# Low parts one turn later on VectorE, Tanh a slot behind the taps, and two places for the levels of the inverse

## The reference

```python
# first block
x = x + hybrid_mixer(x)     # 8 heads gated delta rule + 8 heads block attention, w_in, w_out
x = x + cross_attention(x, mem)                 # 4 heads, w_xq, w_xkv, w_xo
x = x + conv_ffn(x)         # (silu(conv3(h @ w_gate) + b) * (h @ w_up)) @ w_down, width 5632
x = rmsnorm(x, final_norm_g)
# second block
x = layernorm(ALPHA * x + mamba2_mixer(x))      # a_w_in, conv4, 8 groups of state space, a_w_out
k, v = shared_kv(x)
x = layernorm(ALPHA * x + swa_mixer(x, k, v))   # b_w_in, window 128, sinks, b_w_out
```

## Time and profile before

| | |
|---|---|
| time, median of 3 runs | 2648.81 us (2643.33 to 2649.91) |
| profiled execution, its own time | 2667.62 us |
| its span | 2665.8 us |
| PE busy | 2538.2 us (95%) |
| DVE busy | 1745.6 us (65%) |
| ACT busy | 1204.4 us (45%) |
| POOL busy | 352.9 us (13%) |
| mean granted TensorE clock | 0.982 |

### The profile page before, as it was taken

The page is one execution under the profiler, slowest core; times in us unless marked ns, Lnnn a source line. Parts: engine busy times, 40 slices in busy tenths (PEclk is TensorE's granted clock), DMA queues, the critical chain, the costliest instruction groups (busy, mean ns, idle before and its releaser), DMA issues.

```text
span 2665.8 us, 51914 instructions
## 1 busy us (share of the span) xinstructions
PE 2538.2 (95%) x21076; PEld 2459.1 (92%) x21076; DVE 1745.6 (65%) x2732; ACT 1204.4 (45%) x1878; POOL 352.9 (13%) x516
## 2 busy tenths in 40 slices
PE   7999999998799999999999999999999998899997
PEld 7999999988799999999999889999999988799896
DVE  6666645675566665665666677777677775466765
ACT  5333334443444444444444454445445443455553
POOL 1122210040110000000001101101101112210002
PEclk9999999999999999999999999999999999799998
DMA  5433335554355556556556554445454444344452
GB/s 210 143 112 111 111 106 176 172 174 141 112 167 187 186 169 206 186 168 204 189 167 186 166 169 153 159 154 177 153 181 143 158 140 138 110 147 148 143 166 87
DMA packets 124503, 418.37 MB, mean 157 GB/s; under 512 B 13796, under 2 KB 17644, under 8 KB 124012
## 3 DMA queue, kind: packets, MB, share of 16 engines
q1 hardware_dynamic: 124268, 415.06, 47.9%
HBM read 412.37 MB, written 3.68 MB: 156 GB/s over the span
## 4 chain that ended last, share of the span: by engine, by line
PE 73%; DVE 13%; ACT 7%; issue 5%; POOL 1%; DMA 1%; SPq 0%; ACTq 0%; DVEq 0%; POOLq 0%
PE b L690 22%; PE b L691 21%; PE b L692 21%; DVE WL L1521 4%; ACT WH L1146 3%; DVE t1s L1619 2%; PE b L805 1%; PE b L819 1%; ACT XH L1152 1%; PE b L1035 1%; PE b L662 1%; PE b L669 1%; PE b L816 1%; DMA t1s<-memT 1%; DVE XT L1702 1%
## 5 line engine op out<-in xcount | busy, mean ns | idle before, releaser
L1521 DVE TENSOR_TENSOR WL<-WR,WH 128x1024 fp32r<-128x1024 f32 (+2 forms) x811 | 967.0, 1195 | 502.2 <-ACT WH L1146 498.4
L690 PE MATMUL b<-XH,WH 128*128 128x256 f32 x4224 | 1218.0, 288 | 31.5 <-DVE WL L1521 23.6
L691 PE MATMUL b<-XL,WH 128*128 128x256 f32 x4224 | 1186.6, 281 | 0.0
L692 PE MATMUL b<-XH,WL 128*128 128x256 f32 x4224 | 1186.4, 281 | 0.0
L1146 ACT ACTIVATE WH<-WR 128x1024 fp32r<-128x1024 f32 (+2 forms) x811 | 811.1, 1010 | 510.2 <-PE b L692 504.8
L690 PEld LDWEIGHTS b<-XH,WH 128*128 128x128 f32 x4224 | 808.2, 191 | 49.7 <-issue 40.6
L691 PEld LDWEIGHTS b<-XL,WH 128*128 128x128 f32 x4224 | 803.5, 190 | 4.0 <-issue 3.3
L692 PEld LDWEIGHTS b<-XH,WL 128*128 128x128 f32 x4224 | 803.2, 190 | 0.0
L690 PE MATMUL b<-OH,WH 128*128 128x256 f32 x1680 | 482.8, 287 | 15.2 <-DVE XT L1702 11.7
L692 PE MATMUL b<-OH,WL 128*128 128x256 f32 x1680 | 471.3, 281 | 0.0
L691 PE MATMUL b<-OL,WH 128*128 128x256 f32 x1680 | 471.2, 280 | 0.0
(11 more groups left out here) (368 smaller groups left out, 2192.3 us busy)
## 6 DMA issues: line engine op xcount, KB each, us to landing
WR<-a_w_in SPq DMA_DIRECT2D x160, 512.0 KB, 3.6
WR<-w_in SPq DMA_DIRECT2D x112, 512.0 KB, 3.6
WR<-w_gate SPq DMA_DIRECT2D x88, 512.0 KB, 3.7
WR<-w_up SPq DMA_DIRECT2D x88, 512.0 KB, 3.6
WR<-a_w_out SPq DMA_DIRECT2D x64, 512.0 KB, 3.5
WR<-b_w_in SPq DMA_DIRECT2D x64, 512.0 KB, 3.8
WR<-w_down SPq DMA_DIRECT2D x64, 384.0 KB, 3.5
WR<-w_down SPq DMA_DIRECT2D x64, 320.0 KB, 3.1
```

Source lines behind the costliest of these rows:

```text
L690: mm(ps, WH[:, slot, at:at + P], xh, start=(k == 0), stop=False)
L691: mm(ps, WH[:, slot, at:at + P], xl, start=False, stop=False)
L692: m = mm(ps, WL[:, slot, at:at + P], xh, start=False, stop=(k == p["kt"] - 1))
L1521: dve.tensor_tensor(WL[:, s, 0:n], WR[:, r, 0:n], WH[:, s, 0:n].bitcast(F32), ALU.subtract).then_inc(*dve_w.up(i))
```

## The change

- `split` i on DVE makes `WL` i - 1 instead of `WL` i: the low part of a chunk is written one split later in DVE's order. Weight DMAs are issued up to 4 ahead instead of 5, since `WR` is read one turn longer.
- `XL` of a residual and the low part of an `up` product are written after the *next* evac (`low_parts`), or at the end of the projection.
- A conv has steps `convA`, `gateA`, `cB` instead of `convA`, `cB`: the Tanh is written a slot behind the taps, and ACT waits for the taps there.
- The low parts of heads get a step of their own, `lo`, behind the last one of the task.
- The delta rule's `ao` gets two places (`T2(11)`, `T2(16)`), used in turn; POOL writes level l + 2 in step `b` l, level 2 in `l0` and level 1 in `kk`. The block attention's first user of `T2(16)` waits for that.
- The final norm's row is multiplied by ALPHA once on DVE, and ACT's sixteen scalings are gone.

In the diff, `split` is the DVE's, the Tanh and the step `f` that go are ACT's, and `level` is POOL's.

```diff
-ATT = ["v", "lg", "sm", "sn", None, "bk", "pv", "ns", "nr"]
+ATT = ["v", "lg", "sm", "sn", None, "bk", "pv", "ns", "nr", "lo"]
...
     def pump(self, upto):
         while self.split < upto:
-            while self.issued < self.split + RAW:
+            while self.issued < self.split + RAW - 1:
                 self.step("issue", self.issued)
                 self.issued += 1
...
         self.step("evac", key)
+        self.low_parts()
+        if p["evac"] == "up":
+            self.lows.append(("lowup", key[1]))
+        v = VERSION.get(key[:-1])
+        if v is not None:
+            self.lows.append(("xlow", v, key[-1]))
         if p["evac"] in ("conv", "gate"):
-            self.evacs.append((key, [None, p["evac"] + "A", "cB"]))
+            self.evacs.append((key, [None, "convA", "gateA", "cB"] if p["evac"] == "conv" else [None, "gateA", "cB"]))
...
         def split(i):
 
+            i -= 1
+            if i < 0:
+                return
             n, r, s = chunk_n(i), i % RAW, i % HL
             w.wait_ge(*act_w.of(i))
...
-            w.wait_ge(*dve_cv.of("taps", key))
-            act.activation(th, y, ACT.Tanh, scale=0.5).then_inc(*act_cv.up("th", key))
...
-            elif what[0] == "f":
-                m = what[1]
-                w.wait_ge(*dve_dt.of("x3", m))
-                act.activation(XT[:, m, :], XT[:, m, :], ACT.Copy, scale=ALPHA).then_inc(*act_dt.up("x3", m))
...
+                dve.tensor_scalar(ACC[:, :], RB[:, :], ALPHA, None, ALU.mult).then_inc(*dve_dt.up("rows"))
...
             def level(l):
 
                 w.wait_ge(*dve_gdn.of("AT", pr))
-                if l == 1:
+                if l == 2:
                     w.wait_ge(*pe_gdn.of("l0", pr))
                     w.wait_ge(*dve_gdn.of("TT", pr, 0))
-                else:
-                    w.wait_ge(*pe_gdn.of("a", pr, l - 1))
-                pool.tensor_tensor(u4(ao), u4(at_), rep(cc("lev", l * P, P), 4), mult).then_inc(*pool_gdn.up("ao", pr, l))
+                elif l > 2:
+                    w.wait_ge(*pe_gdn.of("a", pr, l - 2))
+                pool.tensor_tensor(u4(T2(AO[l % 2])), u4(at_), rep(cc("lev", l * P, P), 4), mult).then_inc(*pool_gdn.up("ao", pr, l))
```

More of the change, by code:

```diff
@@ L284, in evac, with low_parts @@
             self.begin(("kd", key[1]) if key[1] < 2 else ("vd", key[1]), [None, "rope" if key[1] < 2 else "t"])
+    def low_parts(self):
+        for what in self.lows:
+            self.step(*what)
+        self.lows = []
     def pair(self, name, m, src, kt):
@@ L422, in make_plan @@
     n = len(q.chunks)
-    q.steps = [s for s in q.steps if s[0] not in ("issue", "split") or s[1] < n]
+    q.steps = [s for s in q.steps if s[0] not in ("issue", "split") or s[1] < n + (s[0] == "split")]
     return q
@@ L1231, in gate_a @@
         def gate_a(key):
-            n = plan.products[key]["n"]
-            w.wait_ge(*dve_ev.of(key))
+            p = plan.products[key]
+            n = p["n"]
+            if p["evac"] == "conv":
+                w.wait_ge(*dve_cv.of("taps", key))
+            else:
+                w.wait_ge(*dve_ev.of(key))
             conv_places(n)
@@ L1700, in evac @@
                     w.wait_ge(*dve_ev.of(("bo", 0, m)))
-                v = version(key)
                 dve.tensor_tensor(XT[:, m, :], XT[:, m, :], ps, ALU.add).then_inc(*dve_ev.up(key))
-                if v is not None:
-                    x_low(v, m)
             elif kind == "kv":
@@ L1831, in gdn @@
                 dve.tensor_tensor(Z, Z, from_bank("nr")[:, :], ALU.mult).then_inc(*dve_gdn.up("Z2", pr, frees=releases("nr")))
-                w.wait_ge(*dve_gdn.of("Z2", pr))
+            elif name == "lo":
                 for j in range(2):
@@ L1897, in att @@
                     *dve_att.up("Z2", pr, frees=("att", pr, "nr", "nr")))
-                w.wait_ge(*dve_att.of("Z2", pr))
+            elif name == "lo":
                 for j in range(2):
@@ L1944, in xat @@
                 dve.tensor_copy(o, bank("xat", h, "o", "o")[:, 0:S]).then_inc(*dve_xat.up("o", h, frees=("xat", h, "o", "o")))
-                w.wait_ge(*dve_xat.of("o", h))
-                store("xat", h, o)
+            elif name == "lo":
+                store("xat", h, T1(4 + h % 2))
         def time(*what):
@@ L1971, in time @@
                 w.wait_ge(*(act_sq.of(3, 15) if m == 15 else pool_sq.of(3, m)))
[L1972 to L1973 removed]
+                w.wait_ge(*dve_dt.of("rows"))
+                dve.scalar_tensor_tensor(XT[:, m, :], XT[:, m, :], pc("final_g", m), ACC[:, :], ALU.mult,
                                          ALU.mult).then_inc(*dve_dt.up("x3", m))
@@ L2043, in ssm @@
                         *dve_ssm.up("y4", g, i, frees=releases("nr") if i == 3 else None))
-                    w.wait_ge(*dve_ssm.of("y4", g, i))
-                    store("ssm", 4 * g + i, y)
+            elif name == "lo":
+                for i in range(4):
+                    store("ssm", 4 * g + i, T2(YY[i // 2])[:, half(i % 2)])
         def rot(name):
@@ L2321, in gdn @@
                 pool.tensor_tensor(h2(T1(QD)), second(Q), h2(T1(EG)), mult).then_inc(*pool_gdn.up("qd", pr))
+                level(1)
             elif name == "l0":
-                level(1)
-            elif name[0] == "b" and name != "b6":
-                level(int(name[1]) + 1)
+                level(2)
+            elif name[0] == "b" and int(name[1]) < 5:
+                level(int(name[1]) + 2)
             elif name == "ns":
```

48 lines of the change are left out of this document (27 added, 21 removed).

## The result

| | before | after |
|---|---|---|
| time, median of 4 runs | 2649.4 us (2643.3 to 2673.0) | 2559.7 us (2558.4 to 2566.4) |
| ratio | | 0.965, 95% interval 0.959 to 0.971 |
| profiled execution, its own time | 2667.6 us | 2558.4 us |
| mean granted clock | 0.982 | 0.989 |

A forecast was written before the change was run, and what follows sets the result against it. The PE was taken as the bound, busy 2538 of 2666 us, its pauses caused by late DVE work; terms summed to -58, so 2648.8 - 58 = 2591 us, own range 2580 to 2606, 8 in 10 range 2560 to 2622.

The forecast's parts named there:

- the other pace: Rival: the feed-forward network falls into the faster matmul pace, 31 us go besides, 2560 us; chance 0.14.
- cross attention's projection: Eight pairs of products: DVE waits before WL and XL go, period from 5.27 to 3.39 us, -15 us.
- delta rule, four rounds: The PE's wait for the inverse's first level goes, since it is made a slot before l0: -8.5 us.
- start, first 80 us: First low part comes later, PE starts some 4 us later but catches up: +1 us, between 0 and +4.
- second block's start, 1480 to 1556: Four products lose two DVE waits of 1.44 us each before WL; 11.5 at most, taken as -8 us.
- new waits for low parts: State space part and delta rule: low parts made a turn later come too late, +5 us, between 0 and +12.
- clock, behind cross attention: Three windows partly at 1.2 GHz lost 14 us; half returns as pauses shorten: -7, between 0 and -14.
- The memory: Beside the output projection: DVE's wait before XL goes, the PE becomes the bound, -6.5 us.
- half the gain: Rival: removed waits turn into waits on the DVE's own work, each term halves, 2620 us; chance 0.12.
- POOL and the DVE: Delta rule: WL slows beside POOL's level, counted as nothing; by the skill's contention rule it would be +4 us.
- Low parts too late: Rival: in delta rule and state space projections WL ends after the PE wants it, 2658 us; chance 0.05.
- The slower pace: Rival: the 4990 matmuls of 1560 to 2150 take the slower pace, 25 us come back, 2616; chance 0.10.

The follow-up runs named there:

- the second profile of before: The kernel before run and profiled once more, unchanged; measured 2649.3 us.
- both lags without the levels: Kernel before with low parts of chunks a turn behind and of x, up values and heads a step behind; 2575.7, 2582.4, 2587.6 and 2605.4 us.

## Why the prediction was off

**The pace.** The 52 runs of before that came with these results fall into 34 from 2637 to 2653 (median 2644.3) and 18 from 2670 to 2677 (2673.4). The ten of after fall into six from 2556 to 2566 (2559.0) and four from 2585 to 2588 (2587.6). Like against like the change brings 85.3 and 85.8 us, a ratio of 0.968 both times. Between the two first profiles lie 109 us, of which 27.2 are the network. The prediction laid its difference of 58 on a median that was of the shorter pace, while its profile was of the longer one. That did no harm, as the sum was made of stages beside the network. The rival "the other pace" was priced at 31 us of gain for a network that in the median run had that pace already; that the time came out at its 2560 is chance. Its mechanism, that the network keeps the pace with which it starts, is shown.

**The sum.** This is the step that failed: the terms add up to -58, and beside the network the profiled executions differ by 82 us (91 with the second profile of before). By its terms:

| term | forecast | measured | |
|---|---|---|---|
| cross attention's projection | -15 | -12.5 | `WL` 1.75 us there, not 1.23 |
| stages 536 to 700 (memory, waits of attention) | -8.5 | -8.5 | equal by luck, see below |
| delta rule, four rounds | -8.5 | -14.7 | -24.2 against the second profile of before |
| start, first 80 us | +1 | -3.6 | |
| second block's start, 1480 to 1556 | -8 | -15.4 | with its clock |
| last state space group | -6 | -9.6 | with its clock |
| rest of the state space part | -4 | -2.4 | |
| window attention | -5 | -7.9 | |
| bkv to the second norm, 2210 to 2345 | -2 | -4.2 | with its clock |
| new waits for low parts | +5 | none | |
| clock, behind cross attention | -7 | -3.8 | the rest in the stages |
| 392 to 536, and the tail | 0 | +0.5 | |

Most of the waits named were the right ones: the residual add, the first level and the rotated q went, and the periods of 3.55 and 5.96 us lie in the bands given (3.3 to 3.6, 5.7 to 6.8). One was not, the memory's. The terms mis-sized:

*The second block's start*, the largest miss. Four times the two waits were 11.5 us, and I took 8 because the PE was idle for only 9.4. But 6.8 us of that stretch ran at 1.2 GHz, at half speed, which lengthens the PE's own work by up to 3.4 us; 9.4 and 3.4 make 12.8, and 12.9 went. Another 2.5 us went from 1480 to 1512, where the sum had nothing; undoing the chunk's turn brings 2.3 of them back.

*The memory.* I had -6.5 for it and -2 for the other chains of attention. Measured are -2.1 from 536 to 600 and -1.6 from 600 to 650, and -4.8 from 650 to 700, where the chains of cross attention stand. The wait before `XL` that I took out of the period came back before the next row, and the PE still waits 5.7 of 6.8 us for POOL. The wait moved to another name, as the rival of half the gain had it, and the -8.5 of the two terms is luck.

*The clock.* I counted 14 us of lost full speed in three windows and took half. Over the whole execution the stretches at 1.2 GHz shrank from 95 to 55 us, which is up to 20 us of full speed, and the windows of the earlier trace rows are back at 1.00. I had read three windows and not the rest: there were stretches of 3.4 us before 80 us and in the last delta round, which went, and 9 of the 39 us from 2210 to 2345 went too. The 6.8 us from 600 to 650 stayed. The rule from the Trainium skill that I weighed, page TensorE: Matmul & The Clock Gate (Part 1), by which the full 14 return if the pauses go, was nearer than my half, though the pauses did not go entirely.

*New waits.* I had worked out 0.3 us too late for one chunk in the state space part, "if the DVE gains nothing on the way". The DVE's waits for `WH` fell by 479 us, and the `WL` waits of the PE fell from 13.0 to 4.1 beside the start instead of rising by 5.

*The start.* First matmul +3.4 as forecast (4), then -7.0 instead of about -3: the stretch at 1.2 GHz at 45 us went; it is there again when the chunk's turn is undone. Kept early, the start gives 2.3 more.

*The delta rule.* I took the wait of 8.5 us and called nothing late behind it. The four rounds take 312.1 and 321.6 us in the two profiles of before. The levels alone make that 304.5, both lags without the levels 313.7, all edits but the levels 318.4, and all together 297.4: the lags pay here only together with the levels. How much of the gain is the clock's depends on the profile of before, which had 3.4 us at 1.2 GHz in these rounds in one execution and 23.9 in the other.

*POOL and the DVE*, for which I wrote nothing. In cross attention's projection six of the `WL` take 0.53 us longer each, 3.2 us in all, which is what that term stayed behind its -15 and a little more. The Trainium skill's page GPSIMD Engine Reference (Key points) names such contention; by it I had weighed +4 in the delta rule, which the sum left out, and no such loss is seen there.

The rivals: half the gain did not come as a whole, since where the DVE is the next bound its periods are the 3.55 and 5.96 us that had been worked out; beside the memory it did. Low parts too late did not come, for the reason that I gave. The slower pace did not strike the stretch from 1556 to 2150 (591.6 us after, 594.0 before).

What sets the pace inside the PE was not found; the runs show only what turns it over.

## What to carry to other kernels

Where one in-order engine subtracts what another has just made, let it run one piece of work behind; look then for the other waits in the same period: here one lag alone brought 1.3 and the other 8.8 of 12.4 us, and beside the memory a wait of 0.58 us only moved to the next row. Then look again at whoever was hidden by the old wait: without the second place for POOL's levels the lags brought nothing that can be told in the delta rule (313.7 us, against 312.1 and 321.6), and with it the rounds fell to 297.4. And before two profiles are compared, put their dense stages side by side: 6116 equal matmuls in 693 or in 720 us are no effect of the change.

## What the hardware showed

- At a granted clock of 1.00, dense 128x128x256 matmuls follow each other every 113.3 or every 117.7 ns. The state lasts over thousands of them (692.8 or 720.0 us for 6116). One fp32 matmul of 128x128 between them turned it over in each of 11 places of one execution and in the one or two places of the others. By their times 18 of 52 executions of before and 4 of 10 of after had the longer one.
- The same program can run a stretch at either clock. The second delta round of before, with the same wait of 2.03 us for POOL in both, ran at 1.00 in one execution (78.1 us) and at 0.94 in the other (82.8); with the chunk's turn alone the wait was 3.1 us in the second and in the third round, and the one ran at 0.94, the other at 1.00.
- Where `WL` (128x1024) and a POOL addition of 128x256 meet, the one that began later takes longer. With the addition under way, `WL` took 1.76 us instead of 1.22 and the addition its usual 0.74. With `WL` under way, it kept its 1.22 and the addition took 1.65, in 25 of the 30 additions of line 2272 after the change; in before all 30 (line 2251) took 0.74. That is 24 of the 42 us by which POOL's busy time rose (352.9 to 395.3). It cost nothing: the PE waited 2.7 us for that sum before and after.

```profile
2114.01 1.22 DVE L1541 TENSOR_TENSOR WL<-WR,WH 128x1024 fp32r<-128x1024 f32 x1
2114.18 1.64 POOL L2272 TENSOR_TENSOR ACC<-ACC,XT 128x256 f32<-128x256 f32 x1 [1.16 <-DVE XT L1721]
```
